# Moving v evictions and item copies inside the head-pair pipeline of a four-layer encoder trunk

## The chip, the cores and the metric

The kernel runs on one core of one Trainium2 chip. The metric is the device time of one execution in microseconds (us); lower is better. Each of the three timed runs is one execution.

## The reference

Four residual layers over x of shape (256, 1024) in float32. Layer i mixes tokens in manner i mod 3, then runs a gated MLP with a causal convolution of width 3, then adds an input embedding gated by the residual stream:

```python
for i in range(DEPTH):                      # DEPTH = 4
    h = rms_norm(x, attn_norm[i])
    # i % 3 == 0: forgetting attention (FOX), 16 heads of 64, causal, with cumulative log-forget gates
    # i % 3 == 1: chunked attention with a clipped relative-position bias (REL), 16 heads
    # i % 3 == 2: sliding-window attention, 16 query heads, 2 key/value heads, sinks, rotary (SWA)
    x = x + mixer(h) @ w_o[i]
    x = x + conv_ffn(rms_norm(x, ffn_norm[i]), w_up[i], conv_w[i], conv_b[i], w_down[i])
    gate = sigmoid(rms_norm(x, ple_norm[i]) @ w_ple_gate[i])
    x = x + gate * (p[i] @ w_ple_proj[i])
```

Inside a mixer q and k are RMS-normalised per head, scores are q.k/8 plus a bias or mask, and softmax(scores) multiplies v. So layers 0 and 3 are FOX, layer 1 is REL and layer 2 is SWA.

## The kernel before, in words

**Precision and weights.** Every float32 operand x of a large product is split into a high part (a rounding copy on ScalarE) and a low part x minus high (a subtraction on VectorE), and TensorE forms the product with three matmuls: high-high, high-low, low-high (`three`, L1208). Weights stream in half units of 128x1024 through a ring of four raw buffers. The SP queue loads a half when VectorE has freed its buffer; ScalarE writes `w_hi` (L414), VectorE writes `w_lo` (L697).

**Order of the work.** Each engine has its own program, written out by hand: `block.scalar` (ACT below), `block.vector` (DVE), `block.gpsimd` (POOL), `block.tensor` (PE), `block.sync` (SP). An engine runs its instructions strictly in that order and waits on semaphores that the others raise. There is no planner.

**Projections.** A mixer's input projection is computed in blocks of 512 columns (q0, k0, q1, k1, v0, v1 in FOX and REL) for two token tiles t of 128. A piece is half of the sum over k of one block and one tile: 12 matmuls of 128x512. Pieces 0 to 7 belong to q1 and k1, pieces 8 to 11 to v0, pieces 12 to 15 to v1; piece 10 completes tile 0 of v0, piece 11 tile 1 of v0, piece 14 tile 0 of v1, piece 15 tile 1 of v1. A finished q or k tile is an "item": it is normalised (ACT, DVE, POOL), transposed by PE (`transpose_items`, L1276), and copied from PSUM to `qT`/`kT` as high part (ACT `copy_items`, L502) and low part (DVE `rest_items`, L833 or L835). A finished v tile j (0 to 3 in the order above) leaves PSUM as `v_hi` (ACT `evacuate_v`, L531) and `v_lo` (DVE `rest_v`, L847). The bank of a v tile is used again: piece 12 writes the bank of v tile 0 and waits for it (`v_ready`), piece 13 that of v tile 1, and the first piece of the output projection, `o_piece(0, 0)` (matmuls on L1233), waits until all four v tiles are out.

**The head-pair pipeline** is a loop over steps s. With pair s meaning heads 2s and 2s+1, the engines do in step s of FOX and REL:

- PE: scores of pair s (L1356, in FOX also L1364), the pieces of this step (8 and 9 in step 0; 10 and 11 in step 1; 12, 13, 14, 15 in steps 2, 3, 4, 5; `o_piece(0,0)` in step 6, `o_piece(1,0)` in step 7, `o_piece(0,1)` in step 8), transposes of the probabilities of pair s-1 (L1379), in step 1 the transposes of items 6 and 7, and from step 2 on the products with v of pair s-2 (`values`).
- DVE: masks and row minima of pair s (L939), the low part of the output of pair s-3 (`rest_o`, L973), low parts of items and of v, the reciprocals of the row sums of pair s (`invert_sums`, L959), the low part of the transposed probabilities of pair s-1 (L965), low parts of weights (L697).
- ACT: the high part of the output of pair s-3 (`round_o`, L623), exponentials of pair s (L594), items, v, the high part of the transposed probabilities of pair s-1 (L611), high parts of weights (L414).
- POOL: normalises the probabilities of pair s by the reciprocals (L1158), four operations for a pair.

The scores of pair s+1 wait until the masks of pair s have read the two score banks (`s_min`). The transposes of pair s wait for POOL (`pn_ready`). Dictionaries give the step of each extra: `STEP_V` says that v tiles 0 and 1 leave in step 2, tile 2 in step 5 and tile 3 in step 6, which is one step after the one in which PE finishes them. `STEP_ITEMS` says in which step PE transposes an item; ACT and DVE copy it one step later (`s - 1` in the code). In SWA there is no separate v block; items 4 and 5 are transposed in steps 1 and 2, and `values(0)` and `values(1)` wait for their low parts.

Of the kernel before, what the change touches and what calls it, by code (L numbers as in the profile page):

```python
# [37 lines left out]
FOX, REL, SWA = 0, 1, 2  # L38
# [52 lines left out]
ITEMS_AFTER_PIECE[REL] = ITEMS_AFTER_PIECE[FOX]  # L91
STEP_ITEMS = {FOX: {1: (6, 7)}, REL: {1: (6, 7)}, SWA: {1: (4,), 2: (5,)}}
STEP_O = {FOX: {6: 0, 7: 1}, REL: {6: 0, 7: 1}, SWA: {5: 0, 7: 1}}
STEP_V = {FOX: {2: (0, 1), 5: (2,), 6: (3,)}, SWA: {}}
STEP_V[REL] = STEP_V[FOX]
STEP_SPLITS = {FOX: {1: (16,), 2: (17, 18), 3: (19,), 4: (20,), 5: (21,), 6: (22,), 7: (23,)},
               SWA: {0: (8,), 1: (9,)}}
# [58 lines left out]
def trunk(nc, weights, x_in, p_in, gains, smalls, gainT_in, bf_in, conv, wf_in, rel_in, ident_in, consts_in, out):  # L156
    with ExitStack() as ctx:
# [85 lines left out]
        def item_bank(n):  # L243

            return aux[2 + n % 2]

        def value_bank(pair):
            return aux[2 + pair % 2]

        def pt_bank(h):  # L250
            return acc[2 + h % 2]
# [113 lines left out]
        def item_place(m, n):  # L365

            kind, c, _ = BLOCKS[m][ITEMS[m][n][0]]
            return ((qT_hi, qT_lo) if kind == "q" else (kT_hi, kT_lo)) + (4 * c, 2 if kind == "kv" else 4)

        def item_gain(L, i):  # L370

            which = 0 if BLOCKS[MIXER[L]][ITEMS[MIXER[L]][i][0]][0] == "q" else 1
            return gainT[:, L, which:which + 1]
# [30 lines left out]
        def _(act):  # L404
# [83 lines left out]
            for L in range(DEPTH):  # L488
                m = MIXER[L]
# [5 lines left out]
                def copy_items(*items):  # L495

                    for i in items:
                        n = item0 + i
                        act.wait_ge(qk_tr, n + 1)
                        hi, _, c, k = item_place(m, i)  # L500
                        t = ITEMS[m][i][1]
                        nc.scalar.activation(hi[:, c:c + k, t * P:(t + 1) * P],  # L502
                                             item_bank(n)[:, 0:k * P].rearrange("p (c s) -> p c s", c=k),
                                             ACT.Copy, scale=1.0 if m == SWA else item_gain(L, i)).then_inc(qkT_hi_ready, 1)
# [83 lines left out]
                def exps(h):  # L588

                    g = HEADS * L + h  # L590
                    for qb in range(2):
                        c0, c1 = (0, P) if qb == 0 else (P, 3 * P)
                        act.wait_ge(s_min, 2 * g + qb + 1)
                        nc.scalar.activation(sc[:, h % SC, c0:c1], sc[:, h % SC, c0:c1], ACT.Exp,  # L594
                                             bias=nmax[:, qb, h:h + 1], scale=-1.0,
                                             accum_out=den[:, qb, h:h + 1]).then_inc(p_ready, 1)
# [7 lines left out]
                def round_pT(h):  # L604

                    g = HEADS * L + h
                    pair = h // 2
                    act.wait_ge(pt_done, g + 1)
                    if PAIRS * L + pair >= 2:
                        act.wait_ge(pv_done, PAIRS * L + pair - 1)  # L610
                    nc.scalar.activation(pT_hi[:, pair % 2, h % 2, :], pt_bank(h)[:, 0:3 * P], ACT.Copy).then_inc(pt_hi_ready, 1)  # L611

                def round_o(pair):

                    act.wait_ge(pv_done, PAIRS * L + pair + 1)
                    if m != SWA:

                        act.wait_ge(unit_used, FIRST_IN[L] + (11 if pair < 4 else 12))
                    else:
                        act.wait_ge(unit_used, FIRST_IN[L] + 5)  # L620
                    for e in range(2):
                        r = slice(e * HD, (e + 1) * HD)
                        ins = nc.scalar.activation(hT_hi[r, pair, :], value_bank(pair)[r, e * SEQ:(e + 1) * SEQ], ACT.Copy)  # L623
                    ins.then_inc(o_hi_ready, 1)

                for s in range(PAIRS + 3):
                    if s >= 3:
                        round_o(s - 3)
                    if s < PAIRS:
                        exps(2 * s)  # L630
                        exps(2 * s + 1)
                        if m == SWA:
                            sink_exps(s)
                    for i in STEP_ITEMS[m].get(s - 1, ()):
                        copy_items(i)
                    for j in STEP_V[m].get(s + 0, ()):
                        evacuate_v(j)
                    if 1 <= s <= PAIRS:
                        round_pT(2 * s - 2)
                        round_pT(2 * s - 1)  # L640
                    for j in STEP_SPLITS[m].get(s, ()):
                        split_half(first, j)
                    if s == PAIRS + 1:
                        split_next(FIRST_O[L])
# [44 lines left out]
        def _(dve):  # L689
# [99 lines left out]
            for L in range(DEPTH):  # L789
                m = MIXER[L]  # L790
# [32 lines left out]
                def rest_items(*items):  # L823

                    for i in items:
                        n = item0 + i
                        dve.wait_ge(qkT_hi_ready, n + 1)
                        hi, lo, c, k = item_place(m, i)
                        t = ITEMS[m][i][1]
                        part = (slice(None), slice(c, c + k), slice(t * P, (t + 1) * P))  # L830
                        src = item_bank(n)[:, 0:k * P].rearrange("p (c s) -> p c s", c=k)
                        if m == SWA:
                            ins = nc.vector.tensor_tensor(lo[part], src, hi[part].bitcast(F32), ALU.subtract)  # L833
                        else:
                            ins = nc.vector.scalar_tensor_tensor(lo[part], src, item_gain(L, i), hi[part].bitcast(F32),  # L835
                                                                 ALU.mult, ALU.subtract)
                        ins.then_inc(qkT_ready, 1)

                def rest_v(j):

                    blk, t = VS[m][j]
                    kind, c, _ = BLOCKS[m][blk]
                    src = in_bank(blk, t)
                    dve.wait_ge(v_hi_ready, v0 + j + 1)
                    if kind == "v":
                        cols = slice(c * 512, (c + 1) * 512)
                        ins = nc.vector.tensor_tensor(v_lo[:, t, cols], src[:, :], v_hi[:, t, cols].bitcast(F32), ALU.subtract)  # L847
                    else:
                        for twice in range(2):
                            at = lambda a: a[:, t, 0:256].rearrange("p (h c d) -> p h c d", c=2, d=HD)[:, :, twice, :]  # L850
                            ins = nc.vector.tensor_tensor(at(v_lo), src[:, P:2 * P].rearrange("p (h d) -> p h d", d=HD),
                                                          at(v_hi).bitcast(F32), ALU.subtract)
                    ins.then_inc(v_ready, 1)
# [107 lines left out]
                def rest_pT(h):  # L961

                    pair = h // 2
                    dve.wait_ge(pt_hi_ready, HEADS * L + h + 1)
                    nc.vector.tensor_tensor(pT_lo[:, pair % 2, h % 2, :], pt_bank(h)[:, 0:3 * P],  # L965
                                            pT_hi[:, pair % 2, h % 2, :].bitcast(F32), ALU.subtract).then_inc(pt_ready, 1)
# [10 lines left out]
                if m == SWA:  # L977
                    dve.wait_ge(sink_ready, 1)
                for s in range(PAIRS + 3):
                    if s < PAIRS:  # L980
                        mask_scores(2 * s)
                        mask_scores(2 * s + 1)
                        if m == SWA:
                            sink_sums(s)
                    if s >= 3:
                        rest_o(s - 3)
                    if m == SWA and s < 2:
                        turn_item(4 + s)
                    for i in STEP_ITEMS[m].get(s - 1, ()):
                        rest_items(i)  # L990
                    for j in STEP_V[m].get(s, ()):
                        rest_v(j)
                    if s < PAIRS:
                        invert_sums(s)
                    if 1 <= s <= PAIRS:
                        rest_pT(2 * s - 2)
                        rest_pT(2 * s - 1)
                    for j in STEP_SPLITS[m].get(s, ()):
                        split_half(first, j)
                    if s == PAIRS + 1:  # L1000
                        split_next(FIRST_O[L])
# [564 lines left out]
```

## Time and profile before

| what | us |
|---|---|
| median of 3 runs | 1452.71 |
| lowest, highest run | 1448.46, 1453.45 |
| profiled execution, its own time | 1449.07 |
| its span, first to last instruction | 1447.0 |
| PE busy in the span | 1342.3 (93%) |
| DVE busy | 960.6 (66%) |
| ACT busy | 821.6 (57%) |
| POOL busy | 411.2 (28%) |

The span is the distance from the first to the last instruction of the profiled execution; 2.07 us lie around it. Times in the rows below are us from the start of the span. In layer 0 step 0 of the pipeline begins at 72.4 us, in layer 1 at 434.4, in layer 2 at 787.3.

### The profile page before, as it was taken

The numbers are of one execution on the slowest core, as the hardware profiler recorded it, in microseconds if no ns is written. First come the engines' busy times: TensorE is split into PE (matmuls) and PEld (weight loads), VectorE is DVE, ScalarE is ACT, GpSimd is POOL, SyncE is SP. The second block draws the span as 40 slices with busy tenths as digits, with TensorE's granted clock in tenths as the row PEclk, the third lists the DMA queues.
The fourth block names the chain that finished last, engine by engine and source line by source line (L and its number), as shares of the span: only waits on it lengthen the run. The fifth ranks groups of instructions, "written<-read, shape, count | busy, mean of one in ns | idle before, by whom it ended". The sixth has DMA issues, their size and how long they took to land.

```text
span 1447.0 us, 24524 instructions
## 1 busy us (share of the span) xinstructions
PE 1342.3 (93%) x8340; PEld 1186.1 (82%) x8340; DVE 960.6 (66%) x1449; ACT 821.6 (57%) x1421; POOL 411.2 (28%) x505
## 2 busy tenths in 40 slices
PE   5988999999898899999986699999999789999998
PEld 4766899988776689998875579998877667999886
DVE  4756777754675677775577677776375757777635
ACT  5656666644565666664455566665356656566533
POOL 3432133310164313331017313332004521233200
PEclk9999999999999999999998799999999989999999
DMA  7532555554563255555453045556555324555651
GB/s 273 181 96 74 184 180 178 187 192 170 181 206 113 89 185 179 180 187 193 167 182 118 29 130 176 176 186 191 173 187 170 132 73 151 178 181 179 199 174 59
DMA packets 64022, 232.85 MB, mean 161 GB/s; under 512 B 7280, under 2 KB 7408, under 8 KB 63952
## 3 DMA queue, kind: packets, MB, share of 16 engines
q1 hardware_dynamic: 61056, 221.87, 46.9%
q0 software_dynamic: 2896, 10.05, 2.4%
q8 instruction: 44, 0.72, 0.2%
q14 instruction: 26, 0.21, 0.1%
HBM read 230.84 MB, written 1.05 MB: 160 GB/s over the span
## 4 chain that ended last, share of the span: by engine, by line
PE 70%; DVE 12%; ACT 6%; issue 4%; POOL 4%; DMA 3%; SPq 0%; POOLq 0%; ACTq 0%; DVEq 0%
PE bank L1233 23%; PE bank L1209 15%; PE bank L1210 15%; PE bank L1211 15%; DVE w_lo L697 5%; DMA w_raw<-weights 3%; ACT w_hi L414 2%; DVE tok L744 2%; ACT tok L594 2%; PE bank L1356 1%; PE bank L1379 1%; DVE hT_lo L752 1%; ACT tok L435 1%; POOL hrstd L1063 1%; DVE x L717 1%
## 5 line engine op out<-in xcount | busy, mean ns | idle before, releaser
L697 DVE TENSOR_TENSOR w_lo<-w_raw,w_hi 128x1024 fp32r<-128x1024 f32 x418 | 554.2, 1364 | 145.3 <-ACT w_hi L414 145.0
L414 ACT ACTIVATE w_hi<-w_raw 128x1024 fp32r<-128x1024 f32 x418 | 421.3, 1054 | 157.0 <-PE bank L1233 115.9
L1209 PE MATMUL bank<-hT_hi,w_hi 128*128 128x256 f32 x1408 | 398.8, 283 | 5.8 <-DVE hT_lo L752 5.8
L1210 PE MATMUL bank<-hT_lo,w_hi 128*128 128x256 f32 x1408 | 398.4, 283 | 0.0
L1211 PE MATMUL bank<-hT_hi,w_lo 128*128 128x256 f32 x1408 | 398.4, 283 | 0.0
L1209 PEld LDWEIGHTS bank<-hT_hi,w_hi 128*128 128x128 f32 x1408 | 270.3, 192 | 7.4 <-issue 7.4
L1210 PEld LDWEIGHTS bank<-hT_lo,w_hi 128*128 128x128 f32 x1408 | 270.3, 192 | 0.0
L1211 PEld LDWEIGHTS bank<-hT_hi,w_lo 128*128 128x128 f32 x1408 | 270.3, 192 | 0.0
L1195 POOL TENSOR_TENSOR gate_c<-gate_c,up_c 128x256 f32<-128x256 f32 x88 | 105.0, 1193 | 292.7 <-ACT gate_c L672 292.7
L1209 PE MATMUL bank<-w_hi,hT_hi 128*128 128x512 f32 (+1 forms) x336 | 139.7, 416 | 27.7 <-DVE v_lo L847 16.9
L1030 DVE SCALAR_TENSOR_TENSOR gate_c<-bank,conv_sb,gate_c 128x255 f32<-128x255 f32 (+1 forms) x176 | 84.1, 478 | 121.4 <-ACT up_c L668 121.4
L1210 PE MATMUL bank<-w_lo,hT_hi 128*128 128x512 f32 (+1 forms) x336 | 134.5, 400 | 0.0
L1211 PE MATMUL bank<-w_hi,hT_lo 128*128 128x512 f32 (+1 forms) x336 | 134.0, 399 | 0.0
L1061 POOL TENSOR_SCALAR ssq<-ssq 128x1 f32<-128x1 f32 x24 | 6.0, 250 | 401.6 <-ACT tok L435 401.6
L1233 PE MATMUL bank<-w_hi,gT_hi 128*128 128x512 f32 x352 | 110.9, 396 | 0.0
L1233 PE MATMUL bank<-w_hi,gT_lo 128*128 128x512 f32 x352 | 110.6, 395 | 0.0
L1233 PE MATMUL bank<-w_lo,gT_hi 128*128 128x512 f32 x352 | 110.6, 395 | 0.0
L674 ACT ACTIVATE gT_hi<-gate_c 128x256 f32 (+1 forms) x88 | 36.8, 418 | 122.1 <-POOL gate_c L1195 122.1
L1209 PEld LDWEIGHTS bank<-w_hi,hT_hi 128*128 128x128 f32 x336 | 66.7, 199 | 45.3 <-DVE v_lo L847 17.6
L1197 POOL TENSOR_TENSOR gT_lo<-gate_c,gT_hi 128x256 f32 (+1 forms) x88 | 84.3, 959 | 63.5 <-ACT gT_hi L674 63.5
L1233 PE MATMUL bank<-w_hi,hT_hi 128*128 128x512 f32 x256 | 83.2, 407 | 18.5 <-issue 18.5
L1158 POOL TENSOR_SCALAR tok<-tok,den 128x128 f32<-128x128 f32 (+1 forms) x128 | 55.1, 448 | 130.2 <-DVE den L959 130.0
(136 smaller groups left out, 2026.3 us busy)
## 6 DMA issues: line engine op xcount, KB each, us to landing
w_raw<-weights SPq DMA_DIRECT2D x418, 512.0 KB, 4.1
gain<-gains POOLq DMA_DIRECT2D x11, 512.0 KB, 4.8
rel<-rel_in POOLq DMA_DIRECT2D x8, 256.0 KB, 3.9
x<-x_in SPq DMA_DIRECT2D x2, 512.0 KB, 5.9
p_raw<-p_in POOLq DMA_DIRECT2D x4, 256.0 KB, 5.1
out<-x SPq DMA_DIRECT2D x2, 512.0 KB, 2.6
gain<-gains SPq DMA_DIRECT2D x1, 512.0 KB, 5.8
consts<-consts_in POOLq DMA_DIRECT2D x1, 360.0 KB, 4.5
```

The source lines that it names most:

```text
L414: nc.scalar.activation(w_hi[:, slot, q * HALF:(q + 1) * HALF], w_raw[:, raw, :], ACT.Copy).then_inc(hi_ready, 1)
L594: nc.scalar.activation(sc[:, h % SC, c0:c1], sc[:, h % SC, c0:c1], ACT.Exp, bias=nmax[:, qb, h:h + 1], scale=-1.0, accum_out=den[:, qb, h: ...
L674: nc.scalar.activation(gT_hi[:, k, :], gate_c[:, b, :], ACT.Copy).then_inc(gT_hi_ready, 1)
L697: nc.vector.tensor_tensor(w_lo[:, slot, cols], w_raw[:, half(q)[0], :], w_hi[:, slot, cols].bitcast(F32), ALU.subtract).then_inc(lo_ready, 1)
L1030: ins = nc.vector.scalar_tensor_tensor(buf[:, b, lag:SEQ], up_bank(L, slot)[:, side * SEQ:side * SEQ + SEQ - lag], c[:, 4 * side + tap:4 * ...
L1158: nc.gpsimd.tensor_scalar(sc[:, h % SC, c], sc[:, h % SC, c], den[:, qb, h:h + 1], 1.0, ALU.mult, ALU.mult).then_inc(pn_ready, 1)
L1195: nc.gpsimd.tensor_tensor(gate_c[:, b, :], gate_c[:, b, :], up_c[:, b, :], ALU.mult).then_inc(prod_done, 1)
L1197: nc.gpsimd.tensor_tensor(gT_lo[:, k, :], gate_c[:, b, :], gT_hi[:, k, :].bitcast(F32), ALU.subtract).then_inc(gT_ready, 1)
L1209: nc.tensor.matmul(out_ap, l_hi, r_hi, start=start, stop=False, skip_group_check=True)
L1210: nc.tensor.matmul(out_ap, l_hi, r_lo, start=False, stop=False, skip_group_check=True)
L1211: return nc.tensor.matmul(out_ap, l_lo, r_hi, start=False, stop=stop, skip_group_check=True)
L1233: last = nc.tensor.matmul(banks[2 * t + b][:, :], l[:, c, ts], w[:, slot, col:col + 512], start=(c == 0 and l is left_hi and w is w_hi), s ...
```

## The change

The v tiles of FOX and REL leave earlier: tile 0 in step 1, tile 1 at the very start of step 2 (ahead of the masks on DVE and ahead of the exponentials on ACT), tile 2 in step 4, tile 3 in step 5. The copies of items stand at the end of the step in which PE transposes them, ahead of the step's weight splits. On ACT, `round_o(s - 3)` moves from before the exponentials of pair s to after them; on DVE `rest_o(s - 3)` stays where it was, after the masks and before the reciprocals. PE, POOL and SP are not edited; no instruction is added or removed.

```diff
-STEP_V = {FOX: {2: (0, 1), 5: (2,), 6: (3,)}, SWA: {}}
+BEFORE_STEP_V = {FOX: {2: (1,)}, REL: {2: (1,)}, SWA: {}}
+STEP_V = {FOX: {1: (0,), 4: (2,), 5: (3,)}, SWA: {}}
 STEP_V[REL] = STEP_V[FOX]
@@ block.scalar
                 for s in range(PAIRS + 3):
-                    if s >= 3:
-                        round_o(s - 3)
+                    for j in BEFORE_STEP_V[m].get(s, ()):
+                        evacuate_v(j)
                     if s < PAIRS:
                         exps(2 * s)
                         exps(2 * s + 1)
                         if m == SWA:
                             sink_exps(s)
-                    for i in STEP_ITEMS[m].get(s - 1, ()):
-                        copy_items(i)
-                    for j in STEP_V[m].get(s + 0, ()):
+                    if s >= 3:
+                        round_o(s - 3)
+                    for j in STEP_V[m].get(s, ()):
                         evacuate_v(j)
                     if 1 <= s <= PAIRS:
                         round_pT(2 * s - 2)
                         round_pT(2 * s - 1)
+                    copy_items(*STEP_ITEMS[m].get(s, ()))
                     for j in STEP_SPLITS[m].get(s, ()):
                         split_half(first, j)
@@ block.vector
                 for s in range(PAIRS + 3):
+                    for j in BEFORE_STEP_V[m].get(s, ()):
+                        rest_v(j)
                     if s < PAIRS:
                         mask_scores(2 * s)
                         mask_scores(2 * s + 1)
@@
                         rest_o(s - 3)
                     if m == SWA and s < 2:
                         turn_item(4 + s)
-                    for i in STEP_ITEMS[m].get(s - 1, ()):
-                        rest_items(i)
                     for j in STEP_V[m].get(s, ()):
                         rest_v(j)
                     if s < PAIRS:
@@
                     if 1 <= s <= PAIRS:
                         rest_pT(2 * s - 2)
                         rest_pT(2 * s - 1)
+                    rest_items(*STEP_ITEMS[m].get(s, ()))
                     for j in STEP_SPLITS[m].get(s, ()):
                         split_half(first, j)
```

## Rows read from the trace of the kernel before

**Rows 1.** The page, busy time of each engine in the whole span.
```profile
PE 1342.3 (93%) x8340; PEld 1186.1 (82%) x8340; DVE 960.6 (66%) x1449; ACT 821.6 (57%) x1421; POOL 411.2 (28%) x505
```
**Rows 2.** Waits of PE: who waited <- for whom, us, times, longest.
```profile
PE bank L1233 <- issue: 18.5, 3, 6.6
PE bank L1209 <- DVE v_lo L847: 16.9, 3, 5.8
...
PE bank L1209 <- DVE qT_lo L833: 4.7, 2, 3.1
```
**Rows 3.** PE, order of time, layer 0, step 2 (start, us, instructions, [idle before]).
```profile
94.32 0.80 PE L1209 MATMUL bank<-w_hi,hT_hi 128*128 128x512 f32 x1 [5.57 <-DVE v_lo L847]
...
99.28 0.81 PE L1379 MATMUL bank<-ident,tok 128*128 128x128 f32 x6
...
101.08 0.33 PE L1356 MATMUL bank<-kT_hi,qT_hi 64*128 64x128 f32 x2
```
**Rows 4.** PE, order of time, layer 0, steps 6, 7 and start of 8.
```profile
125.56 1.19 PE L1233 MATMUL bank<-w_hi,hT_hi 128*128 128x512 f32 x2 [5.94 <-issue]
...
130.27 0.82 PE L1379 MATMUL bank<-ident,tok 128*128 128x128 f32 x6
...
132.06 0.33 PE L1356 MATMUL bank<-kT_hi,qT_hi 64*128 64x128 f32 x2
...
133.17 0.73 PE L1233 MATMUL bank<-w_hi,hT_hi 128*128 128x512 f32 x2
...
136.05 0.81 PE L1379 MATMUL bank<-ident,tok 128*128 128x128 f32 x6
...
137.75 0.62 PE L1233 MATMUL bank<-w_hi,hT_hi 128*128 128x512 f32 x2
```
**Rows 5.** DVE, order of time, layer 0: v tiles 0 and 1, and tile 3.
```profile
93.59 1.28 DVE L847 TENSOR_TENSOR v_lo<-bank,v_hi 128x512 fp32r<-128x512 f32 x2
...
124.76 0.69 DVE L847 TENSOR_TENSOR v_lo<-bank,v_hi 128x512 fp32r<-128x512 f32 x1 [0.88 <-ACT v_hi L531]
```
**Rows 6.** Stretches of layers 0, 2: window, length, PE, PEld, DVE, ACT, POOL, clock, DMA.
```profile
94.00:99.20 5.20, 4.88 (x12) 3.87 (x13) 0.95 (x3) 0.00 (x0) 1.62 (x4) 0.53 0.00 0
...
787.30:790.00 2.70, 1.06 (x14) 0.85 (x14) 1.56 (x10) 1.63 (x7) 0.00 (x0) 0.70 0.00 0
```
**Rows 7.** DVE, layer 0: a weight split of step 1; masks of step 4 to step 5.
```profile
88.32 1.23 DVE L697 TENSOR_TENSOR w_lo<-w_raw,w_hi 128x1024 fp32r<-128x1024 f32 x1 [0.30 <-ACT w_hi L414]
...
111.00 0.28 DVE L939 CUSTOM_DVE_ANT_0 tok<-bank,consts 128x128 f32<-128x128 f32 x1
...
112.12 0.85 DVE L973 TENSOR_TENSOR hT_lo<-bank,hT_hi 64x256 fp32r<-64x256 f32 x2
...
113.23 0.18 DVE L959 RECIPROCAL den<-den 128x4 f32<-128x4 f32 x1 [0.26 <-ACT tok L594]
113.75 1.02 DVE L965 TENSOR_TENSOR pT_lo<-bank,pT_hi 128x384 fp32r<-128x384 f32 x2 [0.34 <-ACT pT_hi L611]
...
116.22 0.28 DVE L939 CUSTOM_DVE_ANT_0 tok<-bank,consts 128x128 f32<-128x128 f32 x1
```
**Rows 8.** ACT, layer 0: split of step 1, items of step 2, exponentials and output of step 4.
```profile
87.23 1.06 ACT L414 ACTIVATE w_hi<-w_raw 128x1024 fp32r<-128x1024 f32 x1
...
91.56 1.24 ACT L502 ACTIVATE kT_hi<-bank,gainT 128x512 fp32r<-128x512 f32 x2
...
111.33 0.40 ACT L594 ACTIVATE tok<-tok,nmax 128x128 f32<-128x128 f32 x1 [0.85 <-DVE nmax L939]
...
114.93 0.76 ACT L623 ACTIVATE hT_hi<-bank 64x256 fp32r<-64x256 f32 x2
```
**Rows 9.** POOL, order of time, layer 0: normalisation of pairs 4 (without) and 5 (beside a split).
```profile
113.50 1.62 POOL L1158 TENSOR_SCALAR tok<-tok,den 128x128 f32<-128x128 f32 x4 [3.59 <-DVE den L959]
119.94 2.67 POOL L1158 TENSOR_SCALAR tok<-tok,den 128x128 f32<-128x128 f32 x4 [4.81 <-DVE den L959]
```
**Rows 10.** DVE, order of time, layer 0: the weight split beside it.
```profile
120.78 1.23 DVE L697 TENSOR_TENSOR w_lo<-w_raw,w_hi 128x1024 fp32r<-128x1024 f32 x1
```

## The prediction, made before the changed kernel was run

> **What bounds the kernel now.** I read the page first. PE is busy for 93% of the span and no other engine for more than 66% [rows 1], so the edit pays only through PE's pauses, or through stretches in which PE runs at its lower clock. The waits of PE come next [rows 2]. Two lines stand out with three pauses each: 16.9 us for `v_lo`, and 18.5 us at L1233, the output projection, for which no releaser is named. A third, 4.7 us in two pauses for `qT_lo`, lies in SWA, the only layer with that line. Then PE in order of time. In layer 0 the scores of step 2 end at 88.75, and piece 12 starts at 94.32 after 5.57 us idle [rows 3]. DVE started two v tiles at 93.59 for 1.28 us [rows 5]; half of that ends at 94.23, so tile 0 releases piece 12. The second pause ends at 125.56 [rows 4]; v tile 3 ends at 124.76 + 0.69 = 125.45 [rows 5]. That is the unnamed releaser: `o_piece(0,0)` waits for four v tiles. Three of each kind [rows 2] are one pair in each of layers 0, 1 and 3; layer 1's are the longest of their lines, 5.8 and 6.6, which leaves 5.5 and 6.0 for layer 3.
>
> A pause costs more than its length. Behind the first the granted clock is 0.53, nearly all of it at the lower level, 1.2 GHz [rows 6]: piece 12 takes 99.28 - 94.32 = 4.96 us, while the like piece of step 7 takes 136.05 - 133.17 = 2.88 us at 2.4 GHz [rows 4]. The piece behind the second pause is as slow, 130.27 - 125.56 = 4.7 [rows 4].
>
> **What goes.** Layer 0, step 2: scores end at about 88.7, the transposes of the probabilities start at 99.28, and with the 2.8 us of a full-speed piece they would start at 91.5: 7.8 us. Step 6: scores end at 125.56 - 5.94 = 119.6, transposes at 130.27 against 119.6 + 2.9 = 122.5: 7.8 us. Layer 3 has the same two pauses. Layer 1 has 5.8 + 6.6 and twice 2.1 for the clock: 16.6. Gross: 15.6 + 16.6 + 15.6 = 47.8 us. Of this I expect some 33 us.
>
> **What is late next.** Call M(s) the start of the masks of step s. ACT and DVE form a ring: masks, exponentials, high part of probabilities, weight split on ACT, the same half on DVE, next masks. Before, M(4) = 111.00 and M(5) = 116.22, a turn of 5.22 us [rows 7], below PE's own step of about 5.7 us (132.06 to 137.75 is one, [rows 4]). It was short because `round_o` (114.93, 0.76 us [rows 8]) ran on ACT beside DVE's split and masks. The change puts it into the ring, and makes DVE's `rest_o` and everything behind it (reciprocals, low parts of probabilities, split, masks) wait for it.
>
> From the rows: exponentials start 0.33 us after the masks and end with the reciprocals' start, 113.23 - 111.33 = 1.9 [rows 7, 8]. `round_o` (0.76, seen by DVE about 0.8 on) and `rest_o` (0.85) follow, so the reciprocals come at M + 3.9 instead of M + 2.23 (113.23 - 111.00). What lay between reciprocals and next masks before, 116.22 - 113.23 = 2.99, shrinks to about 2.2 (low parts of probabilities 1.02, split 1.14, a row of 1.23 less its overlap with the next), for ACT has done its part while DVE waited: a turn of 6.1 us. A v tile on DVE (0.61, half of 1.28 less overlap) makes it 6.7 in steps 4 and 5. Step 2 has two splits and no `round_o`: 5.22 + 1.14 = 6.36.
>
> Start of the chain: in step 1 ACT is free for the items at 87.23, they take 1.14 (1.24 less overlap, [rows 8]), the split reaches DVE 1.09 later (88.32 - 87.23, [rows 7, 8]) at 89.46 and takes 1.14, v tile 1 takes 0.61: M(2) = 91.2 (before: 88.32 + 1.15 = 89.5). Then M(3) = 97.6, M(4) = 103.7, M(5) = 110.4, M(6) = 117.1, M(7) = 123.2. Items and v tile 1 thus cost 1.75 us at M(2), covered in step 2, where the scores of step 3 are due at 93.3 and M(2) + 1.2 = 92.4. This cover is 0.9 us thick; beyond it, each later us at M(2) is a us on the ring.
>
> PE against it: step 3 starts at 93.3 (before 101.08 [rows 3]: 7.8 us won), step 4 one full-speed step of 5.8 later at 99.1, step 5 at 104.9 to 105.9, step 6 at 111.6 to 112.6, since it needs M(5) + 1.2. Its scores end at 112.7. `o_piece(0,0)` needs v tile 3, on DVE at M(5) + 3.86 to + 4.5, so 114.97: a new pause of about 2.3 us (before: 5.94). Step 7 starts at 119.65; `o_piece(1,0)` needs `rest_o(3)` at M(6) + 3.9 = 121.0, a pause of 0.3. Step 8 starts at 125.7 against 137.75 [rows 4]: 12.05 us won. In step 8 the transposes of pair 7 wait for POOL: M(7) + 3.86, + 0.27 to start (113.50 - 113.23), + 1.62 = 129.0, while PE is there at 128.5.
>
> POOL's row decides how much: four operations take 1.62 us, but 2.67 where a weight split of DVE (120.78) falls into them (119.94) [rows 9, 10]. With the reciprocals 1.6 us later, POOL's work falls on the split in nearly every step. So I take half to all of 1.05 us in step 8, little elsewhere, as step 5's start is given as a range: 11 us for layer 0, the same for layer 3. Layer 1's gross is 1 us more, but its PE step is shorter (no L1364) while the ring is the same, so it loses as much more: 11.
>
> The Trainium skill, "SBUF — State Buffer", section "Who interferes with whom", states that a DVE instruction with two SBUF inputs contends with a GpSimd instruction that reads SBUF, and that the second to issue blocks fully. `w_lo<-w_raw,w_hi` has two SBUF inputs, and the row of 2.67 us agrees in size. By that rule it speaks against the change: the later reciprocals put POOL and split side by side. If DVE is the one blocked, the ring's turn grows too.
>
> For that no row gives a sure price: the DVE split beside POOL took 1.23 us, like any other [rows 10], so zero below; above, the 1.05 us that POOL lost, in five turns a layer. I take zero, the nearest row.
>
> **SWA (layer 2).** The low parts of items 4 and 5 come before the masks of the next step. `values(0)` loses its 1.6 us pause and `values(1)` its 3.1 us pause [rows 2], with some low clock behind it 5 us by step 4. Then `round_o` lies in the ring here too: reciprocals come 1.6 us later, and where a step has no projection piece to cover that (4 and 6), PE's transposes wait about 1 us more for POOL each. 5 - 2 = 3 us are left; bounds 0 (all given back) and 6 (both pauses, the clock, nothing given back).
>
> **Nothing** is expected from the rest: PE is the bound before and after the pairs, no instruction is added, and SP's queue is fed by splits that keep their step; DMA was idle (0.00) while PE caught up behind both pauses [rows 6].
>
> **Sum.** 11 + 11 + 11 + 3 = 36 us from the profiled execution's 1449.07: 1413.1. The median of the runs lies 3.6 us above that execution, so a median would be 1416.7; I forecast 1415 between the two.
>
> **Rivals.**
> A. The ring costs nothing: reciprocals and copies overlap better than counted and PE runs its own steps. Gross 47.8 + 5 in SWA: 1449.1 - 52.8 + 1.8 = 1398. For it: DVE and ACT have idle time in each step. Against: the dependences are serial. 0.13.
> B. The clock falls again at the new pause of step 6, or the ring turns longer by DVE being blocked. For it: from 787.3 to 790 in SWA PE was idle 1.64 of 2.70 us and the clock fell within it (0.70, [rows 6]). Against: mine is 2.3 us idle in a step of about 7. Price 2.1 us a layer (4.96 - 2.88), 6.3 in all; with 0.5 us in each turn, 2.5 a layer, 7.5 more. 1421 to 1429. 0.25.
> C. The pauses stay because something else releases them. Against: the v tile's end stands 0.1 us ahead of PE in each layer. It would come out within 7 us of before: 1449. 0.03.
> D. Slower. If the many short waits of steps 3 to 8 keep PE at 1.2 GHz, a step takes about 5.7 x 1.8 = 10.3 us (4.96 against 2.88 is 1.7, shorter matmuls are worse), 4.6 more each. From three such steps a layer the gain of 11 is gone; with six it is -17 a layer, near 1500. Against: PE stays over 80% busy in those steps by my count, and layer 2's low-clock stretch has far longer waits. 0.03.
> My own forecast, 1407 to 1421, holds 0.56.
>
> Range 1402 to 1428. A difference of 0.5%, 7.3 us, is about what a measurement of this kernel tells from none: faster by more 0.94, within it 0.03, slower 0.03.
>
> **What would show it.** Right: no wait for `v_lo` at step 2, granted clock 1.00 there; step 3 of layer 0 starting near 93.3; M(s) 6.1 to 6.7 us apart in steps 3 to 7; a pause of about 2.3 us before L1233 in step 6; POOL's four operations at 2.7 us in many steps; step 8 near 126. Wrong: M(s) 5.2 to 5.8 apart (rival A), a clock near 0.5 in step 6 or a turn above 7 us (B), low clock across steps (D).

## The result, and the profile after

| | before | changed |
|---|---|---|
| median of the runs (lowest to highest), 4 each | 1453.01 us (1448.46 to 1453.45) | 1420.97 us (1409.98 to 1421.83) |
| profiled execution (its span) | 1449.07 (1447.0) | 1421.83 (1419.7) |
| mean granted clock of TensorE | 0.969 | 0.981 |

The ratio is 0.9772, 95% interval 0.9747 to 0.9797: the change wins 32 us (1453.01 - 1420.97). The forecast was 1415 with a range of 1402 to 1428, so the median came out 6 us above it. The run of 1409.98 us had a mean granted clock of 0.988, the other three 0.979 to 0.983. The two profiled executions are 27.2 us apart, since that of before was one of its quicker runs and that of the changed kernel its slowest. All line numbers are one to three higher than before (v tiles L849, masks L941, output projection L1236). This is the page of the changed kernel, busy time by engine: the same work, and POOL 11.6 us busier [rows 1].

```profile
PE 1336.5 (94%) x8340; PEld 1179.5 (83%) x8340; DVE 962.4 (68%) x1449; ACT 821.2 (58%) x1421; POOL 422.8 (30%) x505
```

PE of the changed kernel in order of time, layer 0: piece 12 and step 3, which answer to [rows 3], then steps 7 and 8, which answer to [rows 4].

```profile
88.58 0.50 PE L1212 MATMUL bank<-w_hi,hT_hi 128*128 128x512 f32 x1
...
91.46 0.81 PE L1382 MATMUL bank<-ident,tok 128*128 128x128 f32 x6
...
93.26 0.33 PE L1359 MATMUL bank<-kT_hi,qT_hi 64*128 64x128 f32 x2
...
119.32 0.33 PE L1359 MATMUL bank<-kT_hi,qT_hi 64*128 64x128 f32 x2
...
125.02 0.62 PE L1236 MATMUL bank<-w_hi,hT_hi 128*128 128x512 f32 x2
```

Piece 12 starts at once and takes 91.46 - 88.58 = 2.88 us instead of 4.96. Step 3 starts 7.8 us earlier, step 8 12.7 us earlier. All waits of PE that are left between 86 and 131 us, in the same view:

```profile
104.08 0.55 PE L1382 MATMUL bank<-ident,tok 128*128 128x128 f32 x3 [0.56 <-POOL tok L1161]
...
110.94 0.55 PE L1382 MATMUL bank<-ident,tok 128*128 128x128 f32 x3 [0.85 <-POOL tok L1161]
...
114.67 0.70 PE L1236 MATMUL bank<-w_hi,hT_hi 128*128 128x512 f32 x2 [1.02 <-issue]
...
129.51 0.55 PE L1382 MATMUL bank<-ident,tok 128*128 128x128 f32 x3 [1.22 <-POOL tok L1161]
```

The large pauses are gone, and three of the four small ones are waits for POOL's normalised probabilities, for which PE never waited in steps 2 to 8 of before. The windows of the changed kernel (length; PE, PEld, DVE, ACT, POOL; clock; DMA) show the attention stages of layers 0, 1 and 2, and the end of layer 2:

```profile
72.00:135.00 63.00, 59.34 (x382) 48.62 (x381) 44.37 (x123) 43.25 (x116) 24.73 (x38) 1.00 0.31 98
424.00:490.00 66.00, 60.97 (x356) 49.53 (x355) 46.59 (x126) 45.33 (x118) 28.32 (x48) 1.00 0.37 123
764.00:826.00 62.00, 43.97 (x260) 36.20 (x261) 42.29 (x133) 36.00 (x113) 22.22 (x40) 0.78 0.09 29
1057.00:1118.00 61.00, 53.56 (x248) 43.18 (x248) 40.28 (x46) 37.34 (x54) 24.27 (x23) 0.94 0.52 172
```

The same windows of the kernel before, layer 0 and the end of layer 2:

```profile
72.00:144.00 72.00, 60.49 (x370) 49.85 (x370) 42.00 (x121) 42.06 (x114) 20.86 (x38) 0.91 0.27 87
1079.00:1135.00 56.00, 51.35 (x251) 41.52 (x252) 39.35 (x45) 37.36 (x54) 24.75 (x23) 1.00 0.57 187
```

In layer 0 the clock went from 0.91 to 1.00. At the end of layer 2 it went the other way, from 1.00 to 0.94. To see where the time went I cut each trace at the start of a layer's first scores and of its last product with the values:

| us | layer 0 | layer 1 | layer 2 (SWA) | layer 3 | between layers 2 and 3 |
|---|---|---|---|---|---|
| before | 73.41 | 72.81 | 57.66 | 72.85 | 289.87 |
| changed | 62.22 | 61.87 | 58.49 | 62.26 | 294.93 |
| gain | 11.2 | 10.9 | -0.8 | 10.6 | -5.1 |
| forecast | 11 | 11 | 3 | 11 | 0 |

With 0.5 us from the stretches not shown this makes the 27.3 us between the spans. The ring itself is seen on DVE: the masks' starts in steps 2, 3, 4 and 7 of layer 0.

```profile
91.13 0.28 DVE L941 CUSTOM_DVE_ANT_0 tok<-bank,consts 128x128 f32<-128x128 f32 x1
...
97.39 0.28 DVE L941 CUSTOM_DVE_ANT_0 tok<-bank,consts 128x128 f32<-128x128 f32 x1
...
103.60 0.28 DVE L941 CUSTOM_DVE_ANT_0 tok<-bank,consts 128x128 f32<-128x128 f32 x1
...
122.83 0.28 DVE L941 CUSTOM_DVE_ANT_0 tok<-bank,consts 128x128 f32<-128x128 f32 x1
```

Steps 5 and 6 start at 110.11 and 116.61; the turns are 6.26, 6.21, 6.51, 6.50 and 6.22 us, against 5.22 before [rows 7] and some 5.7 that PE wants. In each of steps 3 to 7 DVE waits 1.7 us for `round_o`, and ACT 1.65 to 1.84 us for DVE's masks: they wait for each other in turn. Here is DVE in step 3:

```profile
100.27 0.86 DVE L975 TENSOR_TENSOR hT_lo<-bank,hT_hi 64x256 fp32r<-64x256 f32 x2 [1.70 <-ACT hT_hi L624]
```

The loss in SWA, in PE's order of time: the transposes of the probabilities of steps 3 and 4, the output projection of step 5, and that of step 7.

```profile
788.80 0.55 PE L1382 MATMUL bank<-ident,tok 128*128 128x128 f32 x3 [0.63 <-DVE pT_lo L967]
...
794.59 0.55 PE L1382 MATMUL bank<-ident,tok 128*128 128x128 f32 x3 [2.49 <-POOL tok L1161]
...
798.79 1.22 PE L1236 MATMUL bank<-w_hi,hT_hi 128*128 128x512 f32 x2
...
803.76 0.82 PE L1382 MATMUL bank<-ident,tok 128*128 128x128 f32 x6
...
810.61 0.70 PE L1236 MATMUL bank<-w_hi,hT_hi 128*128 128x512 f32 x2 [1.35 <-DVE hT_lo L975]
```

The pauses for `qT_lo` (3.1 and 1.6 us) went, but the transposes of step 4 now wait 2.49 us for POOL, the projection behind them takes 803.76 - 798.79 = 4.97 us at the lower clock instead of 2.88, and step 7 waits 1.35 us.

### The profile page after: what moved, and what is told of

Same layout as the page of the kernel before. It is cut to its first block, busy times and chain, and to the rows that moved or that the text cites. A ratio compares the mean times of both kernels' runs of the same rounds, so it can differ in the third digit from the quotient of the medians.

```text
span 1419.7 us, 24524 instructions
## 1 busy us (share of the span) xinstructions
PE 1336.5 (94%) x8340; PEld 1179.5 (83%) x8340; DVE 962.4 (68%) x1449; ACT 821.2 (58%) x1421; POOL 422.8 (30%) x505
## 4 chain that ended last, share of the span: by engine, by line
PE 69%; DVE 13%; ACT 5%; POOL 4%; issue 4%; DMA 3%; SPq 0%; POOLq 0%; ACTq 0%; DVEq 0%
PE bank L1236 21%; PE bank L1212 15%; PE bank L1213 15%; PE bank L1214 15%; DVE w_lo L699 5%; DMA w_raw<-weights 3%; ACT tok L595 2%; DVE tok L746 2%; ACT w_hi L415 1%; POOL tok L1161 1%; DVE hT_lo L754 1%; ACT tok L436 1%; PE bank L1359 1%; POOL hrstd L1066 1%; DVE hT_lo L975 1%
## 5 line engine op out<-in xcount | busy, mean ns | idle before, releaser
L1236 PE MATMUL bank<-w_hi,gT_hi 128*128 128x512 f32 x352 | 111.0, 396 | 0.0
L1236 PE MATMUL bank<-w_lo,gT_hi 128*128 128x512 f32 x352 | 110.6, 395 | 0.0
L1236 PE MATMUL bank<-w_hi,gT_lo 128*128 128x512 f32 x352 | 110.6, 395 | 0.0
L1161 POOL TENSOR_SCALAR tok<-tok,den 128x128 f32<-128x128 f32 (+1 forms) x128 | 66.9, 543 | 105.0 <-DVE den L961 104.8
L668 ACT ACTIVATE gate_c<-bank,conv_sb 128x256 f32<-128x256 f32 x88 | 49.7, 565 | 71.1 <-PE bank L1214 71.1
```

Source lines behind the costliest of these rows:

```text
L668: nc.scalar.activation(gate_c[:, b, :], up_bank(L, slot)[:, 0:SEQ], ACT.Identity, bias=c[:, 3:4], scale=c[:, 2:3]).then_inc(conv_first, 1)
L1161: nc.gpsimd.tensor_scalar(sc[:, h % SC, c], sc[:, h % SC, c], den[:, qb, h:h + 1], 1.0, ALU.mult, ALU.mult).then_inc(pn_ready, 1)
L1236: last = nc.tensor.matmul(banks[2 * t + b][:, :], l[:, c, ts], w[:, slot, col:col + 512], start=(c == 0 and l is left_hi and w is w_hi), s ...
```

## The experiments

Two theories went into the first set. One: the v tiles and items bring the gain, and `round_o` behind the exponentials takes a part of it back by the longer ring. The other: `round_o`'s place costs nothing that matters, and PE or the clock sets what is left. All kernels below are edits of the changed kernel. "Attention stages" are the times of the table above, for layers 0 to 3. The first four ran together, beside 13 runs of before (median 1452.28), and so did the last four, beside 9 (median 1451.17).

**1. `round_o` back ahead of the exponentials** (`round_o_first`)

```diff
 (ACT, step loop)
+                    if s >= 3:
+                        round_o(s - 3)
                     if s < PAIRS:
                         exps(2 * s)
...
-                    if s >= 3:
-                        round_o(s - 3)
```

> The changed kernel with one part undone: on ACT round_o(s-3) stands ahead of the exponentials again. v tiles and item copies stay where the change put them. Theory 1 (the ring): round_o in the ring masks - exponentials - probabilities - split makes a turn 6.2 to 6.5 us and the reciprocals late, so POOL's four operations fall on DVE's weight split (2.6 us for 1.6) and PE waits 0.6, 0.9, 1.0 and 1.2 us a layer for them. Without it turns fall to 5.2 us (5.7 with a v tile), POOL's groups to 1.6 us, step 8 of layer 0 starts near 122.5 us for 125.0 and PE's four pauses in layers 0, 1 and 3 go: about 3.5 us a layer, and 1 to 3 in SWA; 1409 us against 1421. Theory 2 (what is left to lose is not in the ring but in the item copies ahead of the splits and in low-clock stretches between layers): 1419 to 1423, step 8 of layer 0 at 125.

Measured: 1398.47 us (1395.95 to 1403.42), ratio to before 0.9651 [0.9633, 0.9669], 21 us less than the changed kernel beside it (1419.47). Masks of steps 4 and 5 on DVE of this kernel:

```profile
100.05 0.28 DVE L941 CUSTOM_DVE_ANT_0 tok<-bank,consts 128x128 f32<-128x128 f32 x1
...
105.76 0.28 DVE L941 CUSTOM_DVE_ANT_0 tok<-bank,consts 128x128 f32<-128x128 f32 x1
```

Starts in steps 2 to 7: 88.00, 94.26, 100.05, 105.76, 111.47, 116.67; behind step 2 the turns are 5.79, 5.71 and 5.71 us, which is PE's own step, and then 5.20. All that PE still waits between 86 and 121 us:

```profile
106.51 0.55 PE L1382 MATMUL bank<-ident,tok 128*128 128x128 f32 x3 [0.34 <-POOL tok L1161]
...
109.40 0.70 PE L1236 MATMUL bank<-w_hi,hT_hi 128*128 128x512 f32 x2 [0.19 <-issue]
```

Attention stages 58.62, 57.45, 52.55, 58.68 us: 3.6, 4.4, 5.9 and 3.6 better than the changed kernel. Windows of it over layer 0 and SWA:

```profile
69.20:127.90 58.70, 58.17 (x377) 48.24 (x377) 43.15 (x122) 42.77 (x114) 21.65 (x37) 1.00 0.31 104
753.00:806.00 53.00, 38.41 (x250) 31.85 (x251) 39.45 (x129) 33.20 (x110) 22.26 (x40) 0.81 0.06 21
```

PE is busy 58.17 of 58.70 us in layer 0: no wait is left to win there. The first theory's mechanism holds, but its 1409 us was 10 too high: SWA won 5.9 us where 1 to 3 were expected, and 3.3 to 4.7 lie between layers 2 and 3, where none was. Its path by way of POOL holds in part. POOL's groups fell to 1.64 us in steps 2, 3, 6 and 7, but in the two steps with a v tile they still fall on the split, and PE waits only 0.34 and 0.19 us:

```profile
103.78 2.68 POOL L1161 TENSOR_SCALAR tok<-tok,den 128x128 f32<-128x128 f32 x4 [4.80 <-DVE den L961]
```

This kernel beats both others.

**2. The v tiles alone** (`v_only`): `round_o` as in 1, and the items' copies one step later, as before.

```diff
 (ACT; the same on DVE with rest_items)
+                    copy_items(*STEP_ITEMS[m].get(s - 1, ()))
...
-                    copy_items(*STEP_ITEMS[m].get(s, ()))
```

> Only the v tiles are moved; item copies stand one step later and round_o ahead of the exponentials, as in the kernel before. Theory 1: the pauses at piece 12 and at the output projection go, and the ring has its short turn, but values(0) waits 1.7 us for item 6 and round_o(0) holds the exponentials of step 3 until piece 13 is done; step 8 of layer 0 near 124.6 us, 12 to 14 us won in each of layers 0, 1 and 3, nothing in SWA: 1410 to 1416 us, so no slower than the whole change. Rival: the item copies ahead of the masks are what lets the v tiles pay (values(0) needs them), without them the pause only moves: under 7 us a layer, 1430 or more.

Measured: 1413.22 us (1407.99 to 1418.04), ratio 0.9739 [0.9716, 0.9761]; attention stages 60.25, 59.32, 59.18, 60.24. In layer 0 PE has a new wait, for an item:

```profile
90.81 0.47 PE L1212 MATMUL bank<-pT_hi,v_hi 128*128 128x512 f32 x1 [1.39 <-DVE kT_lo L837]
```

So the v tiles alone win 39.1 us (1452.28 - 1413.22). That is 6 us more than the whole change beside it (1419.47); the intervals of the two ratios just touch, but the four attention stages are 5.9 us shorter in the traces too. Against experiment 1 the items' earlier copies add 14.8 (1413.22 - 1398.47), of which 6.6 us lie in SWA's attention stage and 5.1 in the others' (1.6 + 1.9 + 1.6).

**3. The change without the v tiles** (`v_late`)

```diff
-BEFORE_STEP_V = {FOX: {2: (1,)}, REL: {2: (1,)}, SWA: {}}
-STEP_V = {FOX: {1: (0,), 4: (2,), 5: (3,)}, SWA: {}}
+BEFORE_STEP_V = {FOX: {}, REL: {}, SWA: {}}
+STEP_V = {FOX: {2: (0, 1), 5: (2,), 6: (3,)}, SWA: {}}
```

> The changed kernel with the v tiles back in steps 2 (0 and 1), 5 and 6; items and round_o stay moved. Both theories: the two pauses a layer and the low clock behind them come back. Theory 1: with round_o in the ring they are longer than before by what the ring adds ahead of v tile 3 in step 6, some 1 to 3 us a layer: 1450 to 1460 us, slower than the kernel before or the same. Rival (items and round_o have a gain of their own): under 1445.

Measured: 1457.13 us (1452.15 to 1459.08), ratio 1.0032 [1.0018, 1.0047]: by itself the rest of the change is a small loss. Attention stages 75.48, 74.3, 57.1, 75.23. The pauses are back, and the second is 1.9 us longer than before [rows 4]: counted from the layer's first scores, v tile 3 ends 1.4 us later (54.4 against 53.0) by the longer ring, and PE is there 0.4 us earlier:

```profile
91.76 0.79 PE L1212 MATMUL bank<-w_hi,hT_hi 128*128 128x512 f32 x1 [5.33 <-DVE v_lo L849]
...
124.71 1.19 PE L1236 MATMUL bank<-w_hi,hT_hi 128*128 128x512 f32 x2 [7.80 <-issue]
```

The clock behind them, in windows of this kernel, is low as in [rows 6]:

```profile
88.00:96.00 8.00, 4.24 (x10) 3.37 (x11) 2.88 (x12) 2.82 (x10) 1.62 (x4) 0.57 0.21 66
124.50:134.00 9.50, 9.29 (x44) 7.53 (x45) 2.78 (x8) 1.91 (x4) 1.63 (x4) 0.70 0.00 1
```

**4. The changed kernel again** (`after_again`), beside the other three.

> The changed kernel once more, for the spread of its times: its runs were 1421.8, 1410.0, 1421.5 and 1420.4 us. If the 11 us between them are low-clock stretches that come in some executions only (in the profiled one one of 6.8 us in the projection of layer 3 behind a late weight transfer, which the kernel before did not have), the profile of a shorter run lacks one or more of them and a longer one has them; if they are another thing, the clock's record is the same in both.

Measured: 1419.47 us (1414.24 to 1420.61), ratio 0.9771 [0.9753, 0.9789]. Attention stages 62.26, 61.92, 58.52, 63.80; the stretch between layers 2 and 3 again long, 293.52, with the same 6.8 us at the lower clock. No shorter execution of the kernel has a trace, so the two cannot be compared.

**5. Only the reciprocals ahead of `rest_o`** (`recip_early`). Is it the late reciprocals (and with them POOL beside the split) that cost, or ACT's order itself?

```diff
 (DVE)
-                    if s >= 3:
-                        rest_o(s - 3)
...
                         invert_sums(s)
+                    if s >= 3:
+                        rest_o(s - 3)
```

> The changed kernel, with rest_o on DVE moved behind the reciprocals (round_o on ACT stays after the exponentials). It tells the two prices of round_o's place apart. Theory 1a (the turn of the ring): masks to masks stays 6.2 to 6.5 us, v tile 3 stays as late, step 7 of layer 0 starts at 119.3 from scores at 72.4 as now; only the wait for POOL in step 8 goes (POOL's groups back to 1.6 us): first scores to last values 61.0 us in layers 0 and 3 for 62.2, in SWA, where nothing but POOL's wait is left, 54 for 58.5; 1412 to 1416 us. Theory 1b (the late reciprocals and POOL beside the split are the price): 58.6 us in layers 0 and 3, as with round_o first; 1400 to 1406 us.

Measured: 1412.7 us (1409.69 to 1416.68), ratio 0.9735 [0.9717, 0.9754]; attention stages 63.45, 63.0, 55.9, 62.31. POOL on this kernel is back at 1.63 us wherever its four operations stand in one group:

```profile
104.64 1.63 POOL L1161 TENSOR_SCALAR tok<-tok,den 128x128 f32<-128x128 f32 x4 [6.12 <-DVE den L961]
...
111.76 1.63 POOL L1161 TENSOR_SCALAR tok<-tok,den 128x128 f32<-128x128 f32 x4 [5.50 <-DVE den L961]
```

Yet layer 0 got no shorter, and SWA less so than expected (55.9 for 54). The total lies in the range of the first alternative (1412 to 1416) by luck: its gain came in SWA and between layers 2 and 3. The expectation for layer 0 (61.0) missed, because in the steps with a v tile DVE meets that tile first, and it waits for ACT, where the tile stands behind `round_o`; the reciprocals queue behind it:

```profile
103.77 0.69 DVE L849 TENSOR_TENSOR v_lo<-bank,v_hi 128x512 fp32r<-128x512 f32 x1 [2.31 <-ACT v_hi L532]
104.38 0.17 DVE L961 RECIPROCAL den<-den 128x4 f32<-128x4 f32 x1
104.46 0.83 DVE L975 TENSOR_TENSOR hT_lo<-bank,hT_hi 64x256 fp32r<-64x256 f32 x2
```

The turns are 6.25, 5.86, 7.13, 7.13 and 6.28 us. PE waits 0.59 us for the masks and 1.86 us at `o_piece(0,0)`, and there the clock fell:

```profile
108.00:113.00 5.00, 2.55 (x20) 2.13 (x20) 2.64 (x12) 4.53 (x14) 1.24 (x4) 0.78 0.31 105
113.00:120.00 7.00, 7.00 (x38) 5.68 (x37) 5.10 (x17) 4.32 (x13) 2.01 (x5) 0.67 0.26 76
```

So POOL's contention could be taken away without a gain in layers 0, 1 and 3, while ACT's order stayed. How much of the price there is the late reciprocals' this run doesn't tell, for in the two steps with a v tile they came late all the same; in step 3, which has none, the turn fell from 6.21 to 5.86 us, and to 5.79 in experiment 1. Step 6 has none either and kept its turn (6.28 for 6.22); there ACT waits 0.45 us for PE's transposes. In SWA, which has no v tiles, this kernel wins 2.6 of the 5.9 us (58.5 to 55.9), but the clock has a part in it: 20.5 us of its stage ran at the lower clock, for 27.3 in the changed kernel. Experiment 3 has the changed kernel's order there and 20.5 us too, and took 57.1 us, so some 1.2 are the reciprocals'. Between layers 2 and 3 this kernel took 292.13 us, 1.4 to 2.8 less than the changed kernel's three traces.

**6. Only the items** (`items_only`): the edits of 1 and 3 together.

> Only the item copies are moved to the end of the step of their transposes; v tiles and round_o as in the kernel before. Theory 1: in FOX and REL the copies leave step 2's v tiles 0 and 1 no earlier (items before, then the split, then masks), the two pauses stay: first scores to last values 72.5 to 74 us in layers 0 and 3 (before 73.4, 72.9). In SWA the pauses at values(0) and values(1) go: 52.5 us for 57.7. In all 1446 to 1450 us. Rival: items alone cost, as they push masks back: over 1455.

Measured: 1444.63 us (1442.07 to 1450.47), ratio 0.9948 [0.9932, 0.9964], a little under the 1446 to 1450 expected. SWA takes 52.58 us against 57.66 before: the items win 5.1 us there, the size that I had put on them. The other attention stages stay at 73.79, 71.46, 73.44 us. Against 3, `round_o`'s place costs 0.8% here too (1.0032 - 0.9948), 12 us.

**7. `round_o` first, and POOL in SWA** (`swa_pool`): the last item's norm and turn on POOL go behind the normalisation of pair 0, on which PE waits 10.6 us.

```diff
-                    for i in range(3, len(ITEMS[m])):
+                    for i in range(3, len(ITEMS[m]) - 1):
...
+                    if m == SWA and s == 0:
+                        item_rstd(len(ITEMS[m]) - 1)
+                        turn_item(len(ITEMS[m]) - 1)
```

> A better version: the changed kernel with round_o first, and in SWA POOL normalises pair 0 before it turns item 5 (which PE needs one step later). In the kernel with round_o first PE waits 10.65 us for that at step 1 of SWA. Expected: transposes of pair 0 some 6 us earlier, of pair 1 about 2 us earlier, since item 5's turn and pair 1 then follow: SWA's first scores to last values 50.5 us for 52.5; 1394 to 1397 us, against 1398.5. Rival (PE's wait is only moved to pair 1): 52.5 and no difference.

Measured: 1398.6 us (1397.84 to 1401.47), ratio 0.9645 [0.963, 0.966], the same as 1 within the intervals; the expected 1394 to 1397 was missed. SWA itself takes 50.79 us, as expected (50.5). Its waits on PE:

```profile
763.74 1.70 PE L1385 MATMUL bank<-ident,tok 128*128 128x128 f32 x6 [4.39 <-POOL tok L1161]
...
772.75 1.70 PE L1385 MATMUL bank<-ident,tok 128*128 128x128 f32 x6 [4.88 <-POOL tok L1161]
```

One wait of 10.65 us became two that sum to 9.27. The 1.8 us won in this trace went again between layers 2 and 3 (291.95 against 290.23).

**8. The changed kernel once more, a single execution** (`after_look`): does the loss between layers 2 and 3 belong to the kernel?

> The changed kernel once more, one look. In two profiled executions the projection behind SWA (layer 2 to layer 3) had a stretch of 6.8 us at the lower clock, last values of layer 2 to first scores of layer 3 took 294.9 and 293.5 us; in four kernels without it 289.9 to 290.5. If a late weight transfer and a longer wait of PE at the last norm (1.97 and 2.36 us for 1.13) bring it, a look without the long wait has about 290 us there and a time near 1415; if it belongs to the kernel's code, it is there again.

Measured: 1417.65 us; between layers 2 and 3 293.96 us, the third of three traces of this kernel near 294.

**What happens between layers 2 and 3.** ACT of the changed kernel waits for a weight transfer, and PE, 8 us later, for the transposes' input; then PE's matmuls run at the lower clock:

```profile
1060.17 1.06 ACT L415 ACTIVATE w_hi<-w_raw 128x1024 fp32r<-128x1024 f32 x1 [2.31 <-DMA w_raw<-weights]
```

```profile
1068.65 1.15 PE L1222 MATMUL bank<-ident,tok 128*128 128x128 f32 x8 [2.36 <-DVE tok L746]
...
1070.92 0.79 PE L1212 MATMUL bank<-w_hi,hT_hi 128*128 128x512 f32 x1 [1.11 <-DVE w_lo L699]
...
1072.79 0.63 PE L1213 MATMUL bank<-w_lo,hT_hi 128*128 128x512 f32 x1
```

The same two waits in each trace, with the length of the low-clock stretch behind them and the time between the layers (L1222 is L1219 in before and L1225 in `swa_pool`):

| us | ACT for DMA | PE at L1222 | low clock | between |
|---|---|---|---|---|
| `v_only` | 0.83 | 0.94 | none | 290.0 |
| `round_o_first` | 1.14 | 1.13 | none | 290.23 |
| before | 1.14 | 1.14 | none | 289.87 |
| `v_late` | 1.57 | 1.65 | none | 290.5 |
| `items_only` | 1.54 | 1.73 | none | 290.56 |
| `swa_pool` | 1.59 | 1.73 | 3.4 | 291.95 |
| `recip_early` | 1.71 | 1.79 | 3.4 | 292.13 |
| `after_look` | 1.62 | 1.76 | 6.8 | 293.96 |
| `after_again` | 2.00 | 1.97 | 6.8 | 293.52 |
| changed | 2.31 | 2.36 | 6.8 | 294.93 |

PE's wait follows the transfer's lateness within 0.2 us. The 6.8 us stretches come with waits of 1.76, 1.97 and 2.36 us, yet 1.79 us went with 3.4 and 1.73 us once with none. In each of the ten traces a second wait of PE, 1.11 to 1.18 us for `w_lo`, follows 1.1 us later. The pair is not peculiar to this place: between layers 0 and 1 PE waits 1.88 us at the same line in before, with 3.4 us of lower clock, and 2.48 us in `items_only`, with 6.8 us; there, with another wait of 3.44 us, the stretch took 294.06 us against 288.1 to 289.5 in the other nine traces. So three traces of one kernel agree, but that the change causes its late transfer is not shown. What makes the transfer late was not settled: no experiment moved it by itself. It is also open why one run of the changed kernel took 1409.98 us, as no trace of such a run exists. It had the highest granted clock of the kernel's runs (0.988), but the clock alone does not set the time: a run of experiment 4 at 0.986 took 1419.47 us. (The stretch ahead of the first scores, the same instructions in all ten traces, took 69.2 to 73.6 us, so some of a run's spread comes from there.)

## Why the prediction was right, and where it was not

**Right.** The pauses and their releasers: with the v tiles alone (2) they went, without them (3) they stayed. The gain of 11 us in each of layers 0, 1 and 3 came as 11.2, 10.9 and 10.6, and by the forecast's own path: masks at 91.13, 97.39, 103.60, 110.11, 116.61 and 122.83 where 91.2, 97.6, 103.7, 110.4, 117.1 and 123.2 were given, step 3 at 93.26 (93.3), step 5 at 105.61 (104.9 to 105.9), step 6 at 112.47 (111.6 to 112.6), step 7 at 119.32 (119.65), step 8 at 125.02 (125.7). PE waits for POOL in step 8 by 1.22 us, and POOL's four operations take 2.6 us in steps 3 to 7:

```profile
101.43 2.59 POOL L1161 TENSOR_SCALAR tok<-tok,den 128x128 f32<-128x128 f32 x4 [6.17 <-DVE den L961]
108.25 2.64 POOL L1161 TENSOR_SCALAR tok<-tok,den 128x128 f32<-128x128 f32 x4 [4.22 <-DVE den L961]
```

So the path was right, but its two sizes only in their difference. Gross, experiment 1 wins 14.8, 15.4 and 14.2 us against before, where 15.6, 16.6 and 15.6 were given (44.4 for 47.8), and the ring takes back 3.6, 4.4 and 3.6 where 4.6, 5.6 and 4.6 were implied (11.6 for 14.8). Both were some 3 us too high, and that they cancel is luck.

The pause of step 6 came out at 1.02 us, not 2.3: the terms for POOL that I had spread over "step 5's start is given as a range" fell before it, 0.56 and 0.85 us, so PE reached `o_piece(0,0)` later while v tile 3 came where it was expected (113.88 + 0.69 = 114.57; expected 114.97). These two misses nearly cancel as well. The clock did not fall behind it.

**Wrong by 3.8 us: the SWA term, "5 - 2 = 3 us are left".** The 5 was right: 5.1 in experiment 6. The 2 was the step that failed. I had put "about 1 us more for POOL" on steps 4 and 6; in step 4 PE waits 2.49 us for POOL, where it waits 1.02 us in `items_only` and in experiment 1, so that term was 1.5 us and not far off. What it left out is more: 1.35 us in step 7, where the output projection waits for DVE, and the lower clock, 2.1 us in the projection of step 5 and 1.0 in the matmuls ahead of it (794.59 to 798.79 is 4.20 us, against 820.86 to 824.09, 3.23 us, in `items_only`). Experiment 1 against the changed kernel makes the whole 5.9 us, 6 against 3 4.5. The difference is the clock: `v_late` has the changed kernel's order in SWA and the same wait, but its clock stayed at 1.00, and it is 1.4 us shorter there. Its projections wait for DVE twice (0.79 and 0.78 us), and POOL holds PE in step 6 too. So the ring alone took 4.5 us for the 2, and the clock brought it to 5.9. The same stretch of SWA in the changed kernel and then in `v_late`, and the wait in `v_late`:

```profile
792.00:804.00 12.00, 9.26 (x41) 7.22 (x40) 8.45 (x33) 7.30 (x27) 3.26 (x8) 0.72 0.00 1
```

```profile
815.00:827.00 12.00, 8.46 (x62) 6.76 (x60) 8.35 (x33) 8.28 (x30) 3.25 (x8) 1.00 0.01 1
```

```profile
817.69 0.55 PE L1382 MATMUL bank<-ident,tok 128*128 128x128 f32 x3 [2.51 <-POOL tok L1161]
```

**Wrong by 5 us: "nothing is expected from the rest".** That the same instructions stand there was no reason. The stretch with the late transfer and the clock behind it is 5.1 us longer than in before in the profiled execution, 3.7 and 4.1 in the two others. Together with SWA this is all of the gap between the forecast from the profiled execution, 1413.1, and its 1421.83 (3.8 + 5.1 = 8.9).

**Rivals.** A (the ring costs nothing, 1398) is not what the change did, but it is what its parts can do: experiment 1 measured 1398.47. The price of the ring that I set against the gross, 52.8 - 36 = 17 us, came out as 17.5 in the four attention stages of experiment 1, but only in sum: 11.6 for 14.8 in layers 0, 1 and 3, 5.9 for 2 in SWA. The 21 us of the whole hold 3.3 to 4.7 between layers 2 and 3 besides. The median of 1420.97 us lies on the border between my own 1407 to 1421 and B, which gave nearly the right size (1421 to 1429) at the wrong place: the clock fell again not at step 6 but in SWA and behind it. The turns of layer 0 stayed under 6.6 us, so DVE was not blocked to the extent that B allowed for. C is refuted by experiments 2 and 3, D by the clock of 1.00 in the stages of layers 0 and 1.

**The rule of the Trainium skill** ("SBUF — State Buffer", "Who interferes with whom") was borne out in that POOL and the split slow each other, 1.62 to 2.6 us. That section of the Trainium skill states the full block for DVE's two-port modes and calls the shared pair an exclusive lock in general; the last section shows what single instructions did here. That this is what the change costs is not borne out in layers 0, 1 and 3: in experiment 5 POOL was back at 1.63 us and layers 0 and 1 were no quicker, though the two turns with a v tile were 0.6 us longer there and may hide a small gain, and in experiment 1 two groups of a layer still take 2.68 us. In SWA no group of the changed kernel falls on a split (1.63 us each behind pair 0), so what the late reciprocals cost there is not contention.

## What to carry to other kernels

When engines hand one piece of work around in a ring, a step's length is the sum of what stands in it, not the load of an engine: put what is ready early (here `round_o`) into the slot in which its engine waits for the ring, not between two links of it. Price a pause together with the clock behind it, and price a moved wait again in each stage with other cover: the same 0.76 us in each step cost 3.6 to 4.4 us in a stage full of PE work and 4.5 to 5.9 us in one with gaps. And time the parts of a change one by one: here one of three was a loss of 21 us inside a gain of 32.

## What the runs showed of the hardware

A weight split of DVE and POOL's normalisation hold each other up one instruction at a time. POOL's group is four instructions of 0.36 to 0.49 us. In each of the 15 groups of the changed kernel that meet a split, three keep that length and one takes 1.36 to 1.45 us: the one that starts while the split runs (0.07 to 0.29 us after its start), and it ends 0.24 or 0.35 us after the split's end. In experiment 1 an instruction that started 0.02 to 0.04 us ahead of the split was the one held up. DVE's split took 1.21 or 1.22 us when it began 0.73 us into POOL's group (two of layer 0's five), and 1.37 us when it began 0.87 or 0.88 us into it (three), 0.07 us after POOL's third instruction had started. The whole group loses about 1 us either way. DVE's splits of steps 3 and 5 in the changed kernel, and POOL's fourth instruction of step 3, cut out by a window of its own:

```profile
102.31 1.37 DVE L699 TENSOR_TENSOR w_lo<-w_raw,w_hi 128x1024 fp32r<-128x1024 f32 x1
...
115.48 1.22 DVE L699 TENSOR_TENSOR w_lo<-w_raw,w_hi 128x1024 fp32r<-128x1024 f32 x1
```

```profile
102.59 1.44 POOL L1161 TENSOR_SCALAR tok<-tok,den 128x256 f32<-128x256 f32 x1
```

The clock forgives some pauses and not others of the same length. Behind 1.02 us idle at 114.67 it stayed at 1.00, as it did between layers 2 and 3 behind 1.65 and 1.73 us in two traces. It fell within 1.86 us (with 0.59 us shortly before) in experiment 5, and 0.9 us after the 2.36 us before layer 3. In SWA it fell 1.9 us after a wait of 2.49 us in the changed kernel, and not at all behind 2.51 us at the same place in `v_late`. Waits of 1.73 to 1.79 us went with nothing, 3.4 and 6.8 us of lower clock in four traces, so the length of the last wait does not decide it.
